# Order of the memory and gate projections, of the selection rounds and of one weight split in a two-layer hybrid trunk

## What is computed

```python
x = x + 0.5 * swiglu(rms_norm(x, ffn1_norm), w_gate, w_up, w_down)      # d_ff 2816
h = rms_norm(x, mix_norm)
(dq, dk, dv, iq, ik, iw, gq, gk, gv, gz, ga, gb, mq) = split_columns(h @ w_in)
out_a = dsa_attention(...)      # 6 heads x 64; indexer of 8 heads x 32 picks the top 128 keys of each query
out_b = gdn_mixer(...)          # gated DeltaNet, 6 heads x 64: conv of width 4, silu, chunks of 64, gated RMSNorm with silu(gz)
mem_kv = rms_norm(mem, mem_norm) @ w_mem_kv                              # 256 memory tokens
out_c = memory_attention(mq, mem_kv, ...)                                # 4 heads x 64
x = x + concat(out_a, out_b, out_c) @ w_out
x = x + 0.5 * swiglu(rms_norm(x, ffn2_norm), ...)
```

## Time and profile before

| | |
|---|---|
| Median of 3 runs | 2238.71 us (2238.64 to 2238.83) |
| The profiled execution | 2238.71 us, its span 2236.9 us |
| TensorE busy | 2186.1 us (98%) |
| VectorE, ScalarE, GpSimd busy | 1072.7, 778.1, 369.9 us |
| Mean granted TensorE clock | 0.991 of full speed |
| HBM read | 188.64 MB |

### The profile page before, as it was taken

How to read it: one execution, slowest core, us unless ns; L and a number is a source line. 1 busy time by engine, 2 the same in 40 slices (tenths; PEclk the granted TensorE clock), 3 DMA queues, 4 the chain that set the end, 5 groups by cost and what they waited for, 6 DMA issues and landing times. The chain is left out here.

```text
span 2236.9 us, 33262 instructions
## 1 busy us (share of the span) xinstructions
PE 2186.1 (98%) x13836; PEld 1766.6 (79%) x13836; DVE 1072.7 (48%) x1480; ACT 778.1 (35%) x1054; POOL 369.9 (17%) x311
## 2 busy tenths in 40 slices
PE   8999999999989999999999999999999899999999
PEld 6888888767767788888888888887777677888887
DVE  5334333879636543343343333348795365433322
ACT  5222223473444422322232222235633444222221
POOL 0111013014113411101111111120231034111000
PEclk9999999999999999999999999999999899999999
DMA  5222323221011222223223222332211102222222
GB/s 186 94 94 94 101 90 124 83 95 40 25 63 39 76 94 94 94 89 104 92 98 105 95 94 85 104 133 76 76 41 68 39 20 76 94 98 106 91 94 81
DMA packets 30651, 192.43 MB, mean 86 GB/s; under 512 B 3216, under 2 KB 5392, under 8 KB 11984
## 3 DMA queue, kind: packets, MB, share of 16 engines
q1 hardware_dynamic: 30160, 189.80, 25.1%
q10 hardware_dynamic: 384, 1.07, 0.1%
HBM read 188.64 MB, written 2.10 MB: 85 GB/s over the span
## 5 line engine op out<-in xcount | busy, mean ns | idle before, releaser
L863 PE MATMUL psum<-XH,wh 128*128 128x512 f32 x1904 | 765.7, 402 | 13.2 <-DVE XL L1638 8.4
L865 PE MATMUL psum<-XH,wl 128*128 128x512 f32 x1904 | 745.3, 391 | 0.0
L864 PE MATMUL psum<-XL,wh 128*128 128x512 f32 x1904 | 744.8, 391 | 0.0
L863 PEld LDWEIGHTS psum<-XH,wh 128*128 128x128 f32 x1904 | 359.7, 189 | 102.7 <-issue 13.3
L865 PEld LDWEIGHTS psum<-XH,wl 128*128 128x128 f32 x1904 | 359.3, 189 | 76.6
L864 PEld LDWEIGHTS psum<-XL,wh 128*128 128x128 f32 x1904 | 359.9, 189 | 73.9 <-issue 4.6
L1679 DVE TENSOR_TENSOR wl<-raw,wh 128x2048 fp32r<-128x2048 f32 x88 | 203.2, 2309 | 163.0 <-ACT wh L1333 163.0
L1327 ACT ACTIVATE wh<-raw 128x2048 fp32r<-128x2048 f32 (+1 forms) x92 | 165.8, 1802 | 316.8 <-PE psum L865 316.6
L863 PE MATMUL psum<-HH,wh 128*128 128x512 f32 x704 | 273.9, 389 | 0.0
L864 PE MATMUL psum<-HL,wh 128*128 128x512 f32 x704 | 273.9, 389 | 0.0
L865 PE MATMUL psum<-HH,wl 128*128 128x512 f32 x704 | 273.9, 389 | 0.0
(11 more groups left out here) (252 smaller groups left out, 2132.5 us busy)
## 6 DMA issues: line engine op xcount, KB each, us to landing
raw<-weights SPq DMA_DIRECT2D x143, 1024.0 KB, 5.0
raw<-weights SPq DMA_DIRECT2D x32, 896.0 KB, 4.6
xT<-xt SPq DMA_DIRECT2D x4, 512.0 KB, 6.8
memT<-memt SPq DMA_DIRECT2D x2, 1024.0 KB, 4.9
out<-xT SPq DMA_DIRECT2D x8, 256.0 KB, 6.0
stripsA<-strip_table SPq DMA_DIRECT2D x2, 768.0 KB, 6.4
raw<-weights SPq DMA_DIRECT2D x2, 512.0 KB, 6.9
stripsB<-strip_table SPq DMA_DIRECT2D x2, 512.0 KB, 7.1
```

The source lines that it names most:

```text
L863: pe.matmul(out_ap, a_hi, b_hi, start=first, stop=False)
L864: pe.matmul(out_ap, a_hi, b_lo, start=False, stop=False)
L865: return pe.matmul(out_ap, a_lo, b_hi, start=False, stop=last)
```

## The change

Four things are done. (1) In each layer the units are reordered: mk and mv (units 8 and 9) become units 7 and 8, and the last two gz groups (unit 7) become unit 9; the steps around them are rewritten, `silu_vz` goes behind gz, and the ten selection rounds of the stretch are dealt out anew. (2) In the inversion a `sel` follows the pulled steps rather than coming before them. (3) In slot 0, all four slices of v pulled there stand before `("sum", 3)`, where one did before. (4) Unit 18 is split in one piece at the end of slot 12; before, half its high part was made there, the other half and half the low part in slot 13, the rest in slot 14.

```diff
-MIX_SRC = (["iq", "small"] + [(O_G + 256 * i, 256) for i in range(6)] + ["mk", "mv", (O_MQ, 256)]
+MIX_SRC = (["iq", "small"] + [(O_G + 256 * i, 256) for i in range(5)] + ["mk", "mv", (O_G + 1280, 256), (O_MQ, 256)]
...
-    for c in range(12):
+    for c in range(10):
         g(("gq", "gk", "gv", "gz")[c // 3], 2 + c // 2, "T", c=c % 3, col=128 * (c % 2))
     for c in range(2):
-        g("mk", 8, "M", c=c, col=128 * c)
+        g("mk", 7, "M", c=c, col=128 * c)
     for b in range(2):
-        g("mv", 9, "V", b=b)
+        g("mv", 8, "V", b=b)
+    for c in range(2):
+        g("gz", 9, "T", c=c + 1, col=128 * c)
...
     spread(FIRST_ROUNDS, 2, range(4, 13), 0)
-    per_slot[12] += [("hi", 18, 0, KD // 2)]
+    per_slot[12] += [("hi", 18, 0, KD), ("lo", 18, 0, KD)]
     spread(SECOND_ROUNDS, 1, [*range(13, N_SLOTS - 1), N_SLOTS - 1, N_SLOTS - 1, N_SLOTS - 1], 1)
-    per_slot[13] = [("hi", 18, KD // 2, KD), ("lo", 18, 0, KD // 2)] + per_slot[13]
-    per_slot[14] = [("lo", 18, KD // 2, KD)] + per_slot[14]
...
     norm("sq", *pairs(1))
     put(("idx", 4))
     sel(1)
-    mm("gz", 1)
+    mm("mk", 0)
+    ev("mk", 0)
+    mm("mk", 1)
     factors(1)
-    ev("gz", 1)
+    ev("mk", 1)
     norm("sq", *pairs(2))
     put(("idx", 5))
-    mm("gz", 2)
-    ev("gz", 2)
-    sel(2)
-    mm("mk", 0)
+    mm("mv", 0)
+    ev("mv", 0)
+    mm("mv", 1)
     factors(2)
-    ev("mk", 0)
-    put("silu_vz")
-    mm("mk", 1)
-    ev("mk", 1)
+    ev("mv", 1)
     norm("sq", *pairs(3))
     sel(2)
-    mm("mv", 0)
-    ev("mv", 0)
-    sel(2)
-    mm("mv", 1)
+    mm("gz", 1)
+    ev("gz", 1)
+    sel(3)
+    mm("gz", 2)
     factors(3)
-    ev("mv", 1)
-    sel(2)
+    ev("gz", 2)
+    put("silu_vz")
+    sel(3)
     mm("mq", 0)
     ev("mq", 0)
     put(("vt", 0), ("vt", 1))
...
     for i, step in enumerate(INVERSION):
         order.append(step)
-        if i < len(INVERSION) - 5:
-            sel(1)
         if i < 9:
             pull(0.7 if i < 6 else 1.3)
         else:
             pull(1.02)
         if i == 0:
             put(("vt", 2), ("vt", 3))
+        if i < len(INVERSION) - 5:
+            sel(1)
...
     for p in range(N_SLOTS):
         order.append(("att", p))
+        if p < 2:
+            pull(2.0 if p == 0 else 9.0)
         if p == 0:
-            pull(0.6)
             put(("sum", NB - 1))
-            pull(1.6)
-        if p == 1:
-            pull(9.0)
         if p == 1:
             put(("out", NB - 1), ("hi", 16, 0, KD // 2))
```

## The result

The changed kernel takes 2250.5 us (median of 5 runs, 2247.91 to 2253.46) against 2238.71 us: slower by a factor of 1.0055, 95% interval 1.004 to 1.0069. That is +11.8 us where +6.3 was forecast. The direction and the range (2240 to 2251) hold, the size doesn't: it is nearly twice the forecast. The profiled execution took 2250.33 us, its span 2248.4. The change makes the file three lines shorter from the steps on, so that L863 of before is L860 here, L1146 is L1143, L1266 is L1263.

What follows compares the result with a forecast made beforehand. TensorE, 98% busy, was taken as the bound. Per layer -0.8 + 0 + 1.5 + 2.3 = +3.0, both layers +6.0, with -0.5 for layer 2's inversion and +0.8 for clock: +6.3 on 2238.71, 2245.0 us, range 2240 to 2251.

Steps and rivals of the forecast that it cites:

- What bounds the kernel: Whole kernel: TensorE is busy for 98% of the span, so a change of order can win only from waits and clock.
- edit 1: Projections: the transposes of gv start at 489.4 instead of 490.17, a gain of 0.8 us per layer, bounds 0 to 1.2.
- edit 3: Slot 0: the later sum delays ScalarE's queue and slot 1's logits, costing 1.5 us per layer, bounds 1.0 to 3.2.
- edit 4: Slots 12 to 14: VectorE's whole low part delays the normalising step, costing 2.3 us per layer, bounds 1.1 to 4.0.
- The alternative price of 2.9: Unit 18's low part: sharing a port pair with GpSimd could lengthen it, costing 2.9 instead of 2.3 us per layer.
- edit 2: Inversion: zero booked in layer 1, a gain of 0.5 us in layer 2; bounds -2.5 to +1.5 for both layers.
- the work in front of them is the same sum in another order: Inversion: VectorE's work before LT, AT and Y is unchanged in total, so Y stays at 518.40; zero booked in layer 1.
- most is covered by the pulled matmuls: Inversion: a round of about 1.2 us held back by a waiting copy is mostly hidden behind TensorE's pulled work.
- The clock: Slots 1 and 14: half-clock stretches appearing or lengthening after longer waits, 0.8 us in all.
- half clock spreads: Rival, chance 0.18: the edits in slots 0 and 12 to 14 each add a 1.6 us stretch per layer, 2250.6 us.
- Early waits heal: Rival, chance 0.24: projections and inversion gain their most, slot 0 costs 1.0 per layer, unit 18 2.3; 2240.4 us.
- Faster: Rival, chance 0.08: copies behind selection rounds hold up TensorE throughout the inversion; gains at six of seven norms, 2232.3 us.

Runs made afterwards that it cites:

- edit 2 alone: The kernel before with only the inversion's selection rounds moved behind the pulled steps: 2245.72 us, ratio 1.0032.
- edit 1 alone: The kernel before with only the projections' units, steps and selection rounds reordered: 2236.21 us, ratio 0.9989.
- edits 3 and 4 alone: Two kernels, each the kernel before with one edit: the head sum behind all four slices, 2242.07 us; unit 18 split in one piece, 2244.49 us.

## Why the prediction was wrong, by its own steps

*What bounds the kernel, edit 1, edit 3, edit 4: right.* Edit 1's new waits stand where they were put, 0.73 and 0.52 us; its gain was 1.3 to 1.5 per layer against 0.8; in layer 1 ScalarE's high part took 1.90 us and not 2.1, and its roots were done 0.3 us earlier against the layer's start than counted. Edit 3 gave 1.6 against 1.5. Edit 4 gave 2.7 and 2.8 against 2.3: the value product started 2.1 us later in both layers, and the other 0.6 to 0.7 came behind it, where the half-clock stretch was 3.4 us longer. Its first wait was 2.61 (forecast 3.0), its second 0.70 (forecast "about 2"). XL came 3.04 us behind the normalising step, where 3.1 was forecast, so the second wait was misread in the prediction itself: from its 705.1 to its 708.2 are 3.1 us, and TensorE's work between the two took 1.8 before (702.13 to 703.90), which leaves 1.3. The logits of slot 14 then took 1.52 us at half clock where they had taken 0.92, and that is the rest. The alternative price of 2.9, worked out from the port rule, named the right size for the wrong reason: the whole low part took 2.29 us, just as in a quiet place, while GpSimd had nothing to do.

*The step that failed is edit 2*: "the work in front of them is the same sum in another order", and of a round behind a waiting copy, "most is covered by the pulled matmuls", with +1.5 as the upper bound for both layers. The first half held for the first Y (518.95 against 518.40, the wait of 1.42 down to 0.30, nothing won). The second did not: the loss from the first x on is +2.8 us in each layer, and edit 2 alone costs +7.1 in the median. The round was priced at 1.2 us; the one that matters ends its block and runs 557.36 to 560.22, 2.9 us with its mask. The pulled matmuls don't cover it, because the copy it stands behind ends after them. The edit moves thirty rounds in each layer, and the prediction rests on the timeline around the first ten only. The trace puts the edit's cost at 2.8 us per layer, 5.6 in all, where -0.5 was booked: a miss of 6.1 us, and the whole forecast was short by 5.5.

*The clock was undersized.* 0.8 us was booked; by the rows there are some 9 to 10 us more at 1.2 GHz, at most 5 us of time. Edits 2, 3 and 4 alone each had more of it than the kernel before, edit 1 alone less. The stretch in layer 2 that edit 2 was to remove (0.89 over 1598 to 1630, then 0.95) did go, and the stretch to the first x gained 1.4 us, of which the inversion gave 1.0 back. But that 0.4 agrees with the 0.5 booked by luck: edit 1 alone has the 0.95 and the same gain, and edit 2 alone has 0.89. The rival "half clock spreads" came out nearest in time, 2250.6, but not as it was told. It had one more stretch at edits 3 and 4 in both layers, four in all, and three of them did lengthen; but the two edits together cost 4.3 to 4.4 us per layer where it had 7.0, and the most was lost at edit 2, which it left at the forecast's -0.5.

*The other rivals.* "Early waits heal" has edit 2 giving 2.5 us; alone it costs 7.1. "Faster" needed gains at four norms of the inversion; the trace has the one wait at L985 and then losses.

*What stays open.* Which of the half-clock stretches a given wait brings cannot be said from these runs. Edit 1 lengthened the one at 492 us although it removed waits; edits 3 and 4 alone lengthened theirs by 3.4 us in one layer and by 6.8 in the other; putting the sum first left the wait of 2.06 us at slot 14 of layer 2 as it was, and the stretch there was 6.8 longer. Why the single edits sum to 14.1 and the change gives 11.8 is likewise open: the interval of each ratio is about +-2 us.

## What to carry to other kernels

Moving work on an engine that is never the bound is free only if nothing behind it in that engine's queue is waited for: list every instruction that waits for another engine, and see that what fills its wait stays in front of it. For an edit inside a loop, read the timeline at every iteration that differs (here the sixteenth round with its mask), not at the first. And a wait of the bounding engine is worth looking for in the kernel as it is: shifting eight rounds by one slot took 1.5 us off TensorE's waits in each layer and gave 8.6 us, as four half-clock stretches went or shrank with it, 13.7 us in all; two of the four are not near the moved rounds, so that part can't be planned.

## What the runs showed of the hardware

The same mask operation (TENSOR_SCALAR, 128x384) took 0.36 us at 556.45 and 1.03 us at 559.19. In the slow case GpSimd was in its additions for BT, 557.72 to 560.01 in this row of the changed kernel; in the fast one they started at 556.61, when it was under way. GpSimd's two additions took 2.29 us in the slow case and 2.02 in the fast one.

```profile
557.72 2.29 POOL L787 TENSOR_TENSOR BT<-LT,cst 128x384 f32<-128x384 f32 x2 [6.27 <-PE psum L1128]
```

The Trainium skill, page SBUF — State Buffer, section "SBUF: two separate sides", says that VectorE, in some of its modes, and GpSimd take a port pair for a whole instruction, and the one that comes second is blocked until it is free. The trace agrees: the operation ends at 560.22, just behind GpSimd's end.

TensorE's slow stretches were between 3.4 and 17.1 us long in these traces. A shift of a microsecond or less elsewhere went with changes of 3.4 to 6.8 us in them, which is up to 3.4 us of time, more than the shift itself. The Trainium skill, page TensorE: Matmul & The Clock Gate, section "What's actually happening", has the slow state as the default which activity releases; the runs agree in that the stretch at slot 14 went when the waits of 2.06 us in front of it shrank to at most 0.9 us. They also show that the wait alone doesn't fix its length: with the same 2.06 us in front of it, it was 3.4 us long in the kernel before and 10.2 in the one with the sum first.
